# Gated embedding stage: half of the second input's projection moved ahead of the norm's sums on TensorE

## The reference, cut to what matters

```python
    h = h + 0.5 * _swiglu(_rmsnorm(h, ffn2_norm[i]), ffn2_w_in[i], ffn2_w_out[i])
    gate = jax.nn.sigmoid(_rmsnorm(h, ple_norm[i]) @ ple_w_gate[i])
    h = h + gate * (p[i] @ ple_w_proj[i])
return _rmsnorm(h, final_norm)
```

## Time and profile before

| | |
|---|---|
| median of 3 runs | 1517.85 us (1516.86 to 1518.26) |
| profiled execution, first to last instruction | 1515.1 us |
| TensorE matmuls busy | 1482.7 us, 98% |
| TensorE weight loads busy | 1317.9 us, 87% |
| VectorE busy | 1177.7 us, 78% |
| ScalarE busy | 819.8 us, 54% |
| chain that ended last | 87% TensorE, 7% VectorE, 4% ScalarE |

### The profile page before, as it was taken

How to read it: one execution, slowest core, us unless ns; L and a number is a source line. 1 busy time by engine, 2 the same in 40 slices (tenths; PEclk the granted TensorE clock), 3 DMA queues, 4 the chain that set the end, 5 groups by cost and what they waited for, 6 DMA issues and landing times.

```text
span 1515.1 us, 22326 instructions
## 1 busy us (share of the span) xinstructions
PE 1482.7 (98%) x9258; PEld 1317.9 (87%) x9258; DVE 1177.7 (78%) x1394; ACT 819.8 (54%) x998; POOL 49.6 (3%) x40
## 2 busy tenths in 40 slices
PE   8999999899999999999999899999999999999998
PEld 6888889898888988888888888889888889988886
DVE  6988989689889778889667798888866566786654
ACT  6645354575553575444577665455645445565442
POOL 1000015200000000000000000000000000000000
PEclk9999999999999999999999999999999999999999
DMA  8988955279889559889534398897555555465551
GB/s 286 310 290 285 340 190 167 84 253 309 297 281 324 178 192 305 291 284 310 163 112 142 131 302 291 284 327 247 189 187 181 182 166 168 141 220 179 185 183 66
DMA packets 275972, 341.69 MB, mean 226 GB/s; under 512 B 6931, under 2 KB 256939, under 8 KB 275872
## 3 DMA queue, kind: packets, MB, share of 16 engines
q1 hardware_dynamic: 273904, 334.74, 66.8%
q0 software_dynamic: 1968, 5.54, 1.1%
HBM read 339.18 MB, written 2.63 MB: 226 GB/s over the span
## 4 chain that ended last, share of the span: by engine, by line
PE 87%; DVE 7%; ACT 4%; issue 1%; DMA 1%; DVEq 0%; SPq 0%; ACTq 0%
PE banks L1688 43%; PE banks L1689 22%; PE banks L1620 5%; PE banks L1622 5%; PE banks L1621 5%; DVE w_lo L990 1%; ACT w_hi L533 1%; DVE xn L1061 1%; DVE ada_acc L1108 1%; ACT xs L563 1%; DVE x_res L1134 1%; PE banks L1760 1%; ACT xn L552 1%; DVE xs L1009 1%; DMA ada<-in_ada_w 1%
## 5 line engine op out<-in xcount | busy, mean ns | idle before, releaser
L1688 PE MATMUL banks<-xs,w_hi 128*128 128x512 f32 x1952 | 687.4, 396 | 3.6 <-DVE w_lo L990 3.6
L990 DVE TENSOR_TENSOR w_lo<-raw,w_hi 128x2048 fp32r<-128x2048 f32 (+1 forms) x241 | 538.1, 2237 | 169.3 <-ACT w_hi L533 169.0
L533 ACT ACTIVATE w_hi<-raw 128x2048 fp32r<-128x2048 f32 (+1 forms) x249 | 464.3, 1868 | 217.7 <-PE banks L1689 182.8
L1689 PE MATMUL banks<-xs,w_lo 128*128 128x256 f32 x1952 | 547.9, 281 | 0.0
L1688 PEld LDWEIGHTS banks<-xs,w_hi 128*128 128x128 f32 x1952 | 368.4, 189 | 92.1 <-DVE w_lo L990 4.8
L1688 PE MATMUL banks<-g_pair,w_hi 128*128 128x512 f32 x1056 | 370.4, 393 | 0.0
L1689 PEld LDWEIGHTS banks<-xs,w_lo 128*128 128x128 f32 x1952 | 368.8, 189 | 0.0
L1689 PE MATMUL banks<-g_pair,w_lo 128*128 128x256 f32 x1056 | 294.7, 279 | 0.0
L1688 PEld LDWEIGHTS banks<-g_pair,w_hi 128*128 128x128 f32 x1056 | 197.9, 187 | 47.1
L1689 PEld LDWEIGHTS banks<-g_pair,w_lo 128*128 128x128 f32 x1056 | 197.9, 187 | 0.0
L1108 DVE SCALAR_TENSOR_TENSOR ada_acc<-ada,c_act,ada_acc 128x1152 f32<-128x1152 f32 x124 | 175.3, 1414 | 9.3 <-DMA ada<-in_ada_w 6.5
(11 more groups left out here) (302 smaller groups left out, 1696.0 us busy)
## 6 DMA issues: line engine op xcount, KB each, us to landing
ada<-in_ada_w SPq DMA_DIRECT2D x128, 576.0 KB, 6.5
raw<-in_ffn_wg SPq DMA_DIRECT2D x44, 1024.0 KB, 5.4
raw<-in_ffn_wu SPq DMA_DIRECT2D x44, 1024.0 KB, 5.4
raw<-in_ffn_w_in SPq DMA_DIRECT2D x43, 1024.0 KB, 6.3
raw<-in_ffn_wd SPq DMA_DIRECT2D x32, 1024.0 KB, 5.2
raw<-in_ffn_w_out SPq DMA_DIRECT2D x16, 1024.0 KB, 5.2
raw<-in_ffn_wd SPq DMA_DIRECT2D x16, 768.0 KB, 4.6
raw<-in_attn_w_qkv SPq DMA_DIRECT2D x12, 1024.0 KB, 5.3
```

Of the source, the lines that this page charges most:

```text
L533: act.activation(w_hi[:, s, 0:width(c)], raw[:, s, 0:width(c)], ACT.Copy).then_inc(hi_ready, 1)
L990: dve.tensor_tensor(w_lo[:, s, 0:width(c)], raw[:, s, 0:width(c)], w_hi[:, s, 0:width(c)].bitcast(F32), ALU.subtract).then_inc(lo_ready, 1)
L1688: pe.matmul(o, wh[:, k, m], pair, start=first, stop=False, skip_group_check=True)
L1689: return pe.matmul(o[:, 0:T], wl[:, k, m], pair[:, 0, :], start=False, stop=last, skip_group_check=True)
```

## The change

`over_two` gets the list of output blocks that it is to compute, and gives back its last matmul in place of counting the chunk as done. `ple` on TensorE calls it for blocks 0 to 3 ahead of the norm's sums and for blocks 4 to 7 behind them; the second call counts the chunk. Since the first half now writes banks 0 and 1 ahead of the norm, two waits come with it: for the first four tiles of x, which VectorE reads from banks 6, 7, 0 and 1 in the stage ahead, and for the modulation's reductions, which read bank 0. No other engine's program changes.

```diff
-            def over_two(s, hi, lo, first, last):
+            def over_two(s, hi, lo, nbs):
...
-                for nb in range(KT):
+                for nb in nbs:
...
                         ins = mm3(o, wh[:, j, nb * P:(nb + 1) * P], wl[:, j, nb * P:(nb + 1) * P],
-                                  hi(j), lo(j), first and j == 0 and nb % 2 == 0, last and j == 1)
-                ins.then_inc(chunks_done, 1)
+                                  hi(j), lo(j), j == 0 and nb % 2 == 0, j == 1)
+                return ins
...
             def ple(n):
                 c = BASE[n]
 
-                norm(n, True)
                 pe.wait_ge(ev("p_lo"), 1)
                 arrived(c)
-                over_two(c % SLOTS, lambda j: p_hi[:, j, :], lambda j: p_lo[:, j, :], True, True)
+                pe.wait_ge(x_ready, 8 * (n - 1) + 4)
+                pe.wait_ge(ada_stored, 3 * FFN_NO[n])
+                over_two(c % SLOTS, lambda j: p_hi[:, j, :], lambda j: p_lo[:, j, :], range(4))
+                norm(n, True)
+                over_two(c % SLOTS, lambda j: p_hi[:, j, :], lambda j: p_lo[:, j, :], range(4, KT))\
+                    .then_inc(chunks_done, 1)
```

## The result

Over 20 runs each, the changed kernel has a median of 1520.31 us (1518.62 to 1523.16) and the kernel before of 1517.74 us (1515.70 to 1519.89). The ratio is 1.0019, 95% interval 1.0013 to 1.0026: slower, by 2.6 us in the medians and 2.87 us in the means.

A forecast was written before the change was run, and what follows sets the result against it. TensorE, busy 98%, was taken to bound the kernel, with 0.24 us slack at the second gate chunk. Its start 1.91 us later plus 0.1 us restart gave +2.0 on 1517.85: 1519.85 us, range 1518.0 to 1521.4.

The forecast's parts named there:

- The added waits at nothing: Before the projection's first half: waits for four x tiles and the modulation reductions cost nothing, covered by 6 us.
- The time won on TensorE: Norm sums and projection: the sums run without a wait, so the projection's second half ends 0.8 us earlier.
- The delay behind the sums: Norm chain on ScalarE and VectorE: last tile's passes, logarithm, normalisation and splits of xs all move 2.15 us later.
- the lower bound: Norm chain: a shift of 2.05 us with no restart cost, giving +1.7 us in all.
- G1's late release: Second gate chunk on TensorE: weights released at 518.70, wanted at 515.98; 2.72 us idle, start 1.91 us later.
- The restart: TensorE after the wait before the second gate chunk: starting again adds 0.1 us.
- Nothing downstream gives it back: Later gate chunks and next feed-forward: loads stay covered by some 1.1 us, all else moves by the 2.0 us.
- The clock: Rival: the clock falls in the wait before the second gate chunk, +1.4 us more, 1521.2 us; chance 0.13.
- The new wait of 2.72 us is nearer to the second: Before the second gate chunk: wait likened to an earlier 2.23 us one (clock 1.00), not 4.96 us (0.53).
- a clock near 0.5 behind the wait: Sign that the prediction is wrong: granted clock near 0.5, not 1.00, after the wait before the second gate chunk.
- The clean fill: Rival: the second gate chunk's splits do not decide and the wait before the sums is won: -0.73 us; chance 0.08.

The follow-up runs named there:

- the hoist that undoes the delay: Changed kernel with the second gate chunk's weight split moved ahead of the norm's chain on ScalarE and VectorE: median 1516.97 us, ratio 0.9998 to the kernel before.
- the hoist alone: Kernel before, TensorE's order unchanged, with the second gate chunk's weight split ahead of the norm's chain on ScalarE and VectorE: median 1517.61 us, ratio 1.0000.
- filled kernel: Changed kernel plus two unused constant matmuls on TensorE between the first and second gate chunks: median 1519.70 us, ratio 1.0021 to the kernel before.
- ScalarE's hoist: Changed kernel with the second gate chunk's split ahead of the norm's chain on ScalarE only: median 1517.63 us, ratio 1.0006 to the kernel before.
- two blocks: Changed kernel with two of the projection's eight output blocks ahead of the sums instead of four: median 1517.10 us, ratio 1.0006 to the kernel before.
- eight blocks: Changed kernel with all eight projection output blocks ahead of the sums instead of four: median 1523.51 us, ratio 1.0039 to the kernel before.

## Why the prediction was right and wrong

**The added waits at nothing: right.** The first half starts with no bracket, and the sums 506.72 - 503.84 = 2.88 us later, the predicted 24 x 0.120.

**The time won on TensorE: right.** G0 starts 510.89 - 503.84 = 7.05 us after the first half; predicted were 510.26 - 503.20 = 7.06. With the hoist that undoes the delay, the won 0.8 us appears whole, as 0.84 us.

**The delay behind the sums: right, at the lower bound.** The logarithm starts 508.21 - 503.84 = 4.37 us after the first half, against 2.33 us after the first sum before: 2.04 us later, where I took 2.15 and gave 2.05 as the bound. From the start of tile 7's passes to the logarithm it took 505.53 - 504.79 = 0.74 us before, from a standstill, and takes 508.21 - (506.72 + 4 x 0.216) = 0.63 us now (an estimate: the six passes stand in one row), so the 0.1 us that the bound allowed for is saved.

**G1's late release: right, and shown.** G1 starts 519.25 - 503.84 = 15.41 us after the first half against 13.59 before, 1.82 us later; predicted 1.91. The restart costs 518.61 - 518.39 = 0.22 us for the first start instead of 0.12, as predicted. The recorded wait, 2.51 us against 2.72, is counted from the end of the last matmul, which overlaps what comes after it, and not from when the next could start. Hoisting G1's split on both engines takes the whole cost away, hoisting it on one takes part, and the stage time follows the number of matmuls ahead of the sums. With the clock held the change is worth 1.97 us (39.44 - 37.47), the predicted +2.0.

**Nothing downstream gives it back: right.** The stage time still has all of it at the next stage's norm, and the changed kernel is still 849.73 - 845.73 = 4.00 us behind at the attention stage's wait, the 0.63 ahead of the stage and the 3.33 in it.

**The clock: wrong.** The step that failed is "The new wait of 2.72 us is nearer to the second, which is why the forecast keeps the clock". The mechanism and its price were there as a rival (+1.4 us; measured 1.36 and 1.51), with a chance of 0.13, but the clock fell in two executions of three, and a clock near 0.5 behind the wait is one of the signs that the prediction named for being wrong. Nearness to one row was no ground: one execution had shown one wait of 2.23 us at 1.00, and I took it as how such waits mostly end. The changed kernel's own profile has the same wait of the attention stage, with the clock in the window behind it:

```profile
849.73 0.39 PE L1620 MATMUL banks<-cs_hi,w_hi 128*128 128x256 f32 x1 [2.23 <-DVE cs_lo L1008]
...
851.00:853.00 2.00, 2.00 (x11) 2.00 (x11) 0.00 (x0) 0.48 (x1) 0.00 (x0) 0.50 0.03 8
```

Same place, same 2.23 us, and 0.50 where the earlier trace rows have 1.00. The moved matmuls are not needed for it: in the kernel with the hoist alone, which has TensorE's old order, the clock falls there too:

```profile
847.10 0.58 PE L1620 MATMUL banks<-cs_hi,w_hi 128*128 128x256 f32 x1 [2.23 <-DVE cs_lo L1009]
...
847.00:849.00 2.00, 1.91 (x9) 1.91 (x10) 0.44 (x2) 0.00 (x0) 0.00 (x0) 0.50 0.00 0
```

Over all twelve profiled executions it fell behind this wait in eight and held in four. So the row that the forecast leaned on was one draw of two possible ones, and the rarer one. The Trainium skill (TensorE: Matmul & The Clock Gate, section HAM oscillation — how this bites in real kernels) speaks against waits between bursts of matmuls because the next burst starts at the lower clock. I had left it to a rival for a wait of this length; the traces bear it out for 2.23 us in eight executions of twelve and for 2.51 us in two of three.

The predicted time, 1519.85 us, is close to the median for a half-right reason. Adding 2.0 us for the release and 1.4 us in two executions of three gives 2.9 us, beside 2.87 us measured between the means; but three executions are a thin base for that share, and some of the difference may lie in the clock elsewhere in the kernel. The runs lean the same way: the mean granted clock is 0.9956 over the 20 of the changed kernel and 0.9965 over 47 of the kernel before in other rounds, some 1.3 us of full-clock time over the span (an estimate from rounded clocks). That remains argued, not shown. That the median came so close to the forecast is in part luck: two of three profiled executions carry a fall of 1.4 to 1.5 us that the forecast left out.

**The clean fill: rightly held unlikely.** It takes G1's split out of the chain to get it, which the change does not do.

## What to carry to other kernels

Before you fill a wait on the busiest engine by moving work ahead of it, follow what the delayed instruction releases, engine by engine in queue order, to the next thing that the busy engine needs, and read the slack there: 0.24 us was all, and no wait is recorded for a release that comes just in time. If the slack is short, move the work that stands behind the chain (here G1's split) into the wait of the engine that you delay; of the stage's time, either edit alone was worth nothing or cost 2 to 3.5 us, and both together won 0.84 us, which the runs of the whole kernel could not tell from nothing. A new wait of over 2 us on TensorE is to be priced with and without a fall of the clock, and one row in one profile does not say which of the two it will be.

## What the runs showed of the hardware that I had not expected

**The clock falls behind the same wait in one execution and not in another.** Profiled executions by the length of TensorE's wait and its place; held means a granted clock of 1.00 in the windows behind the wait, fell that it went down to 0.50:

| wait, us | place | clock held | clock fell |
|---|---|---|---|
| 0.78 to 0.79 | before G1, filled kernel | 3 | 0 |
| 1.04 to 1.07 | before G1, ScalarE's hoist; two blocks | 2 | 0 |
| 2.08 | before G0, eight blocks | 1 | 0 |
| 2.23 | attention stage, all kernels | 4 | 8 |
| 2.51 | before G1, changed kernel | 1 | 2 |
| 3.03 | before G1, eight blocks | 0 | 1 |
| 4.95 to 4.96 | near 288 us, all kernels | 0 | 12 |

**It can fall when the engine is already at work again.** In the first profile of the change the window that contains the restart has 0.50; in the next, where G1 starts at 518.49, the window from 519 to 521 still has 0.77, and 0.50 follows only from 521 to 523: matmuls start every 0.12 us up to 520.01, 1.5 us after the restart, and every 0.21 us from 520.18 on. What decides in which execution and when it falls stays open.

**A short wait is cheap and a fallen clock is dear.** The restart costs about 0.1 us, the fall 1.4 to 1.5 us, nearly as much as the late release itself.
